# Half of the middle expert loads issued by ScalarE in a queue of its own, in a one-core mixture-of-experts kernel

## The chip, the cores and the metric

The kernel runs on one core of a Trainium2 chip. The metric is the device time of one execution in microseconds (us); lower is better. TensorE is called PE below, VectorE DVE, ScalarE ACT, GpSimd POOL and SyncE SP. "SPq" and "ACTq" are the queues in which SP and ACT issue DMA transfers.

## The reference

The program is a two-part network over a sequence of 256 rows of width 1024, all in float32. The first part is a layer with three attention-like branches, followed by a mixture of experts; the second part is four feed-forward blocks with two mixing blocks between them. The change is in the mixture of experts, which is this:

```python
N_EXPERTS = N_GROUPS * EXPERTS_PER_GROUP        # 4 * 8 = 32
D_EXPERT = 512
...
for gi in range(N_GROUPS):
    hg = jax.nn.silu(jnp.einsum('nd,edf->nef', x, wg[gi])) * jnp.einsum('nd,edf->nef', x, wu[gi])
    y = y + jnp.einsum('nef,efd->nd', hg * gates[:, gi, :, None], wd[gi])
```

Each expert has three matrices of 2 MB (gate and up 1024x512, down 512x1024), so the 32 experts are 192 MB of weights, and every one of them is read.

## The kernel before

Five programs, one for each engine, are written out by hand and are synchronised by semaphores. The experts are done in eight rounds `q` (0 to 7) of four experts each. A round has six **sets** `s`: 0 and 1 are the two halves of the gate matrices, 2 and 3 those of the up matrices, 4 and 5 those of the down matrices. A set is four loads `j` (0 to 3), one for each expert, of 128 x 2048 float32, 1 MB. This text numbers the sets through: set n is `6 * q + s`, so sets 8 and 9 are the up halves of round 1, sets 10 and 11 its down halves, and there are 48 sets, 192 loads.

What PE does in a round: `up` for sets 6q to 6q+3 (L1058), with `scatter` of the round before (L1140 and L1141) after the first of them; four transposes (L1117); `down` for sets 6q+4 and 6q+5 (L1069). In rounds 0 and 1 a `gather(q + 1)` (L939) and some transposes (L1043) follow, which build the inputs of later rounds; they need no weights. At the end of a set PE signals `("exu", q, s)`: the set is used, and its buffers are free.

What ACT does in a round, in this order: the SiLU of the gate product (L1795), which waits for PE's set 6q+1; the copy of the transposed hidden values `eT` (L1799), which waits for the transposes; in rounds 0 and 1 its half of the gather's evictions (L1774) and four copies of transposed slots (L1804); `hidden_high` (L1786), two instructions, which wait for PE's set 6q+5 and then for DVE.

Loads have fixed buffers. From set 8 to set 40 every load of set n goes into a buffer whose former content belonged to set n-4 (16 buffers in turn), so it can be issued once PE has used set n-4. SP issues all of them in the order of the sets (L3327, in `fetch`), each after its wait:

```python
if ld.prev:
    w.wait_ge(*(ld.prev.release or skey(ld.prev.final, "L")))
```

At the end the buffers are dealt out otherwise: the last load of set 41 and the first of set 42 wait for set 39, and the other three of set 42 for set 40. After set 47 come the first loads of the feed-forward block (`m<-in_ffn_w_in`).

Of the kernel before, what the change touches and what calls it, by code (L numbers as in the profile page):

```python
# [132 lines left out]
def build(nc, a, out, scr):  # L133
    with ExitStack() as ctx:
# [12 lines left out]
        signals, at, prefix = {}, {}, [""]  # L147

        def then_inc(ins, name, *keys, by=1):

            name = prefix[0] + name
            if name not in signals:
                signals[name] = Signal(ctx.enter_context(nc.semaphore(name)))
            s = signals[name]
            s.n += by
            for k in keys:
                at[k] = (s, s.n)
            ins.then_inc(s.sem, by)
# [46 lines left out]
        loads, XL, OL = [], {}, {}  # L205

        def load(dst, src, slot=None, release=None):
            if slot is None:
                kind, n = "raw", NR
                c = counts.get(kind, 0)  # L210
                counts[kind] = c + 1
                slot = (kind, c % n)
            ld = Load(len(loads), slot, tails.get(slot), dst, src, release)
            ld.raw = slots[slot]
            tails[slot] = ld
            loads.append(ld)
            return ld
# [39 lines left out]
        def expert_src(e, s):  # L257

            W = a[("expert_w_gate", "expert_w_up", "expert_w_down")[s // 2]][0, e]
            return W.rearrange("(p h k) n -> p h (k n)", p=128, h=2)[:, s % 2, :]  # L260

        def plan_experts():
            pre = [("pre", i) for i in range(7)]
            order = ex_first[:6] + pre[5:7] + ex_first[6:] + [pre[4], pre[1], pre[0], pre[2]] + ex_raw[:2] + pre[3:4]
            order += ex_raw[2:] + ex_split + (ex_first + ex_raw + ex_split) * 9
            order += ex_raw + ex_first + ex_split[:1] + ex_raw + ex_first
            for q in range(NQ):
                for s in range(6):
                    XL["set", q, s] = [load(lambda r: r, expert_src(4 * q + j, s), order.pop(0), ("exu", q, s))
                                       for j in range(4)]  # L270
            assert not order

        def plan_overflow():
            for e in range(32):
                for s in range(6):
                    OL[e, s] = load(lambda r: r, expert_src(e, s), ("over", s % 2), ("ovu", e, s))
# [16 lines left out]
        def plan_first():  # L293
# [21 lines left out]
            for c4 in range(4):  # L315
                for s in range(2):
# [14 lines left out]
        ld = load(lambda r: r[:, 0:576].rearrange("p (k n) -> p k n", n=72),  # L331
                  win[:, IK:IK + 72].rearrange("(k p) n -> p k n", p=128))
# [43 lines left out]
        s, had = 0, [None] * NH  # L376
# [11 lines left out]
        def skey(p, what):  # L388

            return (what, p.j)  # L390
# [67 lines left out]
        def ST(q):  # L458
            return rv(Sx(q, q + 1)[:, 0])
# [40 lines left out]
        for n in range(4):  # L500
            o = 24864 if n else 39456
# [62 lines left out]
            w.past = had  # L564

        where_is = {}

# [936 lines left out]
        def scalar(e, w):  # L1506
# [3 lines left out]
            def inc(ins, what, *keys):  # L1510
                then_inc(ins, "act_" + what, *keys)

            def taken(ins, *key, also=()):
                then_inc(ins, f"bank{where_is[key]}_act", ("taken", key), *also)

            def got(*key):
                w.wait_ge("full", key)
                return bank[where_is[key]]
# [261 lines left out]
            def hidden_high(q):  # L1780
                for n in range(2):
                    w.wait_ge("full", ("ed", q))
                    w.wait_ge("finf", q, n)
                    if q:
                        w.wait_ge("full", ("ey", q - 1, 1, 1))
                    inc(e.activation(fin[2 * n], sg if n else hgx, ACT.Copy), "moe", ("finH", q, n))  # L1786

            def experts():
                for q in range(NQ):
                    if q == NQ - 1:  # L1790
                        when(e, w, overflow)
                    b = got("eu", q, 0)
                    if q:
                        w.wait_ge("finL", q - 1, 1)
                    taken(e.activation(sg, b[:, :], ACT.Silu), "eu", q, 0, also=[("sg", q)])  # L1795
                    b = got("et", q)
                    if q > 1:
                        w.wait_ge("exu", q - 2, 5)
                    taken(e.activation(eT[q % 2], b[:, :], ACT.Copy), "et", q)  # L1799
                    if q < 2:  # L1800
                        gather(q + 1)
                        for s in range(4 * q, 4 * q + 4):
                            b = got("ST", s)
                            taken(e.activation(ST(s), b[:, 0:256].rearrange("p (t n) -> p t n", t=2), ACT.Copy), "ST", s)  # L1804
                    if q < NQ - 1:
                        hidden_high(q)
                e.activation(eps[:, 3:4], eps[:, 0:1], ACT.Sqrt)

            def overflow():
# [181 lines left out]
            o = 0  # L1991
# [7 lines left out]
            for ap, n in ((a["norm2_g"][0], 8), (a["ffn_norm_2"].rearrange("a b n -> (a b n)"), 32),  # L1999
# [6 lines left out]
                     by=16)  # L2006
# [1305 lines left out]
        def sync(e, w):  # L3312
            split = [0]
            fetched = set()

            def fetch(ld):

                if ld.prev:
                    w.wait_ge(*(ld.prev.release or skey(ld.prev.final, "L")))
                kind, i = ld.slot  # L3320
                if kind == "half" and i % 2 == 0:
                    kind, i = "raw", i // 2
                if ld.slot == ("pre", 6):
                    for h in range(2):
                        then_inc(e.dma_start(ld.raw[h], ld.src[:, 1024 * h:1024 * h + 1024]), "ld_pre6", ("ld", ld.n), by=16)
                else:
                    then_inc(e.dma_start(ld.dst(ld.raw), ld.src), f"ld_{kind}{i}", ("ld", ld.n), by=16)  # L3327
                fetched.add(ld.n)

            def ahead(p):  # L3330
# [95 lines left out]
            for pair in (G["wo"][-4:-2], G["wo"][-2:]):  # L3426
                i = (pair[0].slot + 1) % NH // 2
# [7 lines left out]
            for q in range(NQ):  # L3435
                for s in range(6):
                    if (q, s) == (NQ - 1, 3):
                        when(e, w, overflow)
                    if (q, s) == (NQ - 1, 5):
                        for ld in XL["set", q, s]:  # L3440
                            w.wait_ge(*ld.prev.release)
                        for i in range(2):
                            for ld in XL["set", q, s]:
                                o = slice(1024 * i, 1024 * i + 1024)
                                then_inc(e.dma_start(ld.raw[:, o], ld.src[:, o]), f"ld_{'last' if i else ''}{ld.slot[0]}{ld.slot[1]}",  # L3445
                                         ("ld", ld.n, i), by=16)
                        continue
                    for ld in XL["set", q, s]:
                        if ld.n not in fetched:
                            fetch(ld)  # L3450
            for ld in loads:
                if ld.slot[0] == "raw" and ld.prev and ld.prev.release and not ld.release:
# [103 lines left out]
```

## Time and profile before

| | before |
|---|---|
| median of 3 runs | 2061.39 us (2061.29 to 2061.7) |
| the profiled execution | 2061.97 us |
| its span in the profile | 2060.1 us |
| PE busy | 1919.6 us, 93% |
| DVE busy | 1131.3 us, 55% |
| ACT busy | 903.9 us, 44% |
| bytes read from HBM | 500.07 MB |

The span is the time between the first and the last record of the profile; the execution's own time is 1.9 us more. The experts take roughly the stretch from 617 to 1050 us of the span. There the share of PE's busy time says little, since a matmul that waits in its pipeline counts as busy; what the DMA engines moved in each stretch says more. The time of a load "to landing" runs from the start of its issue to the last of its semaphore increments, so it holds both its place behind other loads and its own transfer.

### The profile page before, as it was taken

The page shows a single profiled execution, that of the slowest core. Times are in us where ns is not written, and L with a number is a line of the kernel's source. Part 1 is how long each engine was busy: PE and PEld are TensorE (multiplying, and loading weights), DVE is VectorE, ACT ScalarE, POOL GpSimd, SP SyncE. Part 2 cuts the span into 40 slices and gives each one's busy share as a digit, 9 for nine tenths or more (in the row PEclk, how much of TensorE's full clock was granted, in tenths as well). Part 3 has the DMA queues.
Part 4 walks back from the last instruction along what each step waited for, and adds up shares of the span by engine and source line. Part 5 has one row for each costly group of instructions (what it writes and reads, how often), then busy time and mean ns, then how long its engine had stood idle before and what let it go on. Part 6 is the DMA issues. An engine that isn't in the chain of part 4 may idle for free.

```text
span 2060.1 us, 30842 instructions
## 1 busy us (share of the span) xinstructions
PE 1919.6 (93%) x12904; PEld 1492.4 (72%) x12904; DVE 1131.3 (55%) x1527; ACT 903.9 (44%) x1288; POOL 124.6 (6%) x101
## 2 busy tenths in 40 slices
PE   9999999999999876666699999999999999999998
PEld 7899988889983311111178888888888888988887
DVE  3778874578662110001156666656666766756666
ACT  4655555544342100000045546545555545675554
POOL 0243331001100000000000000000000000000000
PEclk9999999999999989889999999999999999999999
DMA  9654545678999999999985755544555555525552
GB/s 349 208 166 145 164 149 169 199 250 282 326 390 417 421 421 421 422 421 421 420 310 191 235 185 184 183 164 164 185 192 175 184 185 188 174 92 169 190 184 82
DMA packets 247506, 503.52 MB, mean 244 GB/s; under 512 B 12097, under 2 KB 166338, under 8 KB 223042
## 3 DMA queue, kind: packets, MB, share of 16 engines
q1 hardware_dynamic: 246464, 500.70, 67.7%
q8 instruction: 104, 1.70, 0.4%
q10 hardware_dynamic: 898, 0.80, 0.1%
q14 instruction: 40, 0.33, 0.0%
HBM read 500.07 MB, written 1.06 MB: 243 GB/s over the span
## 4 chain that ended last, share of the span: by engine, by line
PE 72%; DMA 10%; SPq 7%; DVE 6%; ACT 3%; issue 2%; POOL 0%; ACTq 0%; DVEq 0%
PE bank L601 14%; PE bank L662 13%; PE bank L603 13%; PE bank L602 13%; PE bank L664 7%; SPq L3327 7%; DMA m<-in_expert_w_down 4%; DMA m<-in_expert_w_up 4%; PE bank L1058 2%; DVE m L2233 1%; PE bank L1069 1%; DMA m<-in_ffn_w_in 1%; PE bank L939 1%; ACT m L1534 1%; SPq L3445 0%
## 5 line engine op out<-in xcount | busy, mean ns | idle before, releaser
L2233 DVE TENSOR_TENSOR m<-m,m 128x1024 fp32r<-128x1024 f32 x505 | 624.0, 1250 | 281.9 <-ACT m L1534 279.8
L601 PE MATMUL bank<-m,m 128*128 128x256 f32 (+1 forms) x1960 | 660.8, 337 | 6.8 <-DVE m L2233 3.4
L603 PE MATMUL bank<-m,m 128*128 128x256 f32 (+1 forms) x1960 | 646.3, 330 | 0.0
L602 PE MATMUL bank<-m,m 128*128 128x256 f32 (+1 forms) x1960 | 646.0, 330 | 0.0
L1534 ACT ACTIVATE m<-m 128x1024 fp32r<-128x1024 f32 x505 | 524.3, 1054 | 226.3 <-PE bank L603 208.7
L662 PE MATMUL bank<-m,m 128*128 128x512 f32 x1248 | 439.8, 394 | 0.0
L601 PEld LDWEIGHTS bank<-m,m 128*128 128x128 f32 x1960 | 369.3, 188 | 56.4 <-issue 10.1
L603 PEld LDWEIGHTS bank<-m,m 128*128 128x128 f32 x1960 | 369.2, 188 | 36.8
L602 PEld LDWEIGHTS bank<-m,m 128*128 128x128 f32 x1960 | 369.5, 189 | 35.4 <-issue 2.4
L664 PE MATMUL bank<-m,m 128*128 128x256 f32 x1248 | 352.7, 283 | 0.0
L662 PEld LDWEIGHTS bank<-m,m 128*128 128x128 f32 x1248 | 234.4, 188 | 54.0
L664 PEld LDWEIGHTS bank<-m,m 128*128 128x128 f32 x1248 | 234.6, 188 | 1.6
L1058 PE MATMUL bank<-m,m 128*32 128x512 f32 x1024 | 172.8, 663 | 57.0 <-DMA m<-in_expert_w_up 37.3
L1058 PEld LDWEIGHTS bank<-m,m 128*32 128x32 f32 x1024 | 40.0, 119 | 178.7 <-issue 75.6
L1884 ACT ACTIVATE m<-bank 128x256 f32<-128x256 f32 x156 | 59.0, 378 | 162.0 <-PE bank L664 162.0
L1069 PE MATMUL bank<-m,m 128*32 128x512 f32 x512 | 91.2, 671 | 35.1 <-DMA m<-in_expert_w_down 29.2
L2781 DVE TENSOR_TENSOR m<-bank,m 128x256 f32<-128x256 f32 x156 | 65.5, 422 | 59.6 <-ACT m L1884 54.8
L1069 PEld LDWEIGHTS bank<-m,m 128*32 128x32 f32 x512 | 21.7, 120 | 96.9 <-DMA m<-in_expert_w_down 57.0
L2650 DVE SCALAR_TENSOR_TENSOR m<-bank,m,m 128x512 f32<-128x512 f32 x8 | 6.0, 750 | 154.5 <-PE bank L1058 154.5
L2656 DVE TENSOR_TENSOR m<-bank,m 128x512 f32<-128x512 f32 x16 | 10.3, 685 | 140.5 <-PE bank L1069 140.5
L1799 ACT ACTIVATE m<-bank 128x512 f32<-128x512 f32 x8 | 4.8, 597 | 139.8 <-PE bank L1117 139.8
L1871 ACT ACTIVATE m<-m 128x512 fp32r<-128x512 f32 x44 | 27.8, 632 | 58.7 <-DVE m L2803 53.7
(352 smaller groups left out, 1390.7 us busy)
## 6 DMA issues: line engine op xcount, KB each, us to landing
m<-in_ffn_w_in SPq DMA_DIRECT2D x88, 1024.0 KB, 5.2
m<-in_expert_w_up SPq DMA_DIRECT2D x64, 1024.0 KB, 26.5
m<-in_expert_w_gate SPq DMA_DIRECT2D x63, 1024.0 KB, 26.3
m<-in_w_in SPq DMA_DIRECT2D x60, 1024.0 KB, 5.2
m<-in_expert_w_down SPq DMA_DIRECT2D x60, 1024.0 KB, 26.1
m<-in_ffn_w_out SPq DMA_DIRECT2D x44, 1024.0 KB, 4.9
m<-in_ada_w SPq DMA_DIRECT2D x24, 1024.0 KB, 6.5
m<-in_a_w_in SPq DMA_DIRECT2D x16, 1024.0 KB, 5.2
```

What stands on the lines that cost most here:

```text
L601: e.matmul(o, s[0], m[0], start=first, stop=False, skip_group_check=skip)
L602: e.matmul(o, s[0], m[1], start=False, stop=False, skip_group_check=skip)
L603: return e.matmul(o, s[1], m[0], start=False, stop=last, skip_group_check=skip)
L662: e.matmul(b[:, :].rearrange("p (h n) -> p h n", h=2), H, N.both[:, k], start=k == 0, stop=False, skip_group_check=True)
L664: ins = e.matmul(b[:, 0:256], L, N.T[0][:, k, :], start=False, stop=k == 7, skip_group_check=True)
L1058: ins = e.matmul(b[32 * j:32 * j + 32, :], XG(q, q + 1)[:, 0, k, 32 * j:32 * j + 32], block(ld, i), start=k == 0, stop=k == 7, skip_group_ ...
L1069: ins = e.matmul(b[n][32 * j:32 * j + 32, :], eT[q % 2][:, 128 * c + 32 * j:128 * c + 32 * j + 32], ld.raw[:, 1024 * i + 512 * n:1024 * i ...
L1534: inc(e.activation(rv(fit(q.H, q.view.shape)), q.view, ACT.Copy), "h", skey(q, "H"))
L1884: inc(e.activation(fb[6][:, 256 * b:256 * b + 256], k[:, 256:512], ACT.Copy), "ffn", (f"f{z}c", n, c, b))
L2233: inc(e.tensor_tensor(rv(fit(q.L, q.view.shape)), q.view, fit(q.H, q.view.shape), ALU.subtract), "l", skey(q, "L"))
L2781: taken(e.tensor_tensor(o, k[:, 0:256], fb[6][:, 256 * b:256 * b + 256], ALU.add), f"f{n}{z}{c}", b, also=[(f"f{z}a", n, c, b)])
L3327: then_inc(e.dma_start(ld.dst(ld.raw), ld.src), f"ld_{kind}{i}", ("ld", ld.n), by=16)
```

## The change

For sets 8 to 39, loads j = 1 and j = 3 are issued by ACT, in ACT's own DMA queue; SP keeps j = 0 and j = 2 there, and all four of the sets before 8 and from 40 on. ACT issues them at three places in each round, four loads at each: sets 6q+4 and 6q+5 after the SiLU, 6q+6 and 6q+7 after the copy `eT`, and 6q+8 and 6q+9 after `hidden_high`. Each waits for the release of the buffer's former set, as before. Buffers, bytes, sizes and PE's order are as they were. The naming of the landing semaphores is moved into functions that both engines share.

```diff
+        def of_scalar(n, j):
+
+            return 8 <= n < 40 and j % 2 == 1
...
+            def fetch_sets(n0):
+
+                for n in (n0, n0 + 1):
+                    for j in range(4):
+                        if of_scalar(n, j):
+                            ld = XL["set", n // 6, n % 6][j]
+                            done = ld.prev.release
+                            assert 6 * done[1] + done[2] <= n - 4
+                            w.wait_ge(*done)
+                            lands(e.dma_start(ld.raw, ld.src), ld)
+
             def experts():
                 for q in range(NQ):
...
                     taken(e.activation(sg, b[:, :], ACT.Silu), "eu", q, 0, also=[("sg", q)])
+                    fetch_sets(6 * q + 4)
                     b = got("et", q)
                     if q > 1:
                         w.wait_ge("exu", q - 2, 5)
                     taken(e.activation(eT[q % 2], b[:, :], ACT.Copy), "et", q)
+                    fetch_sets(6 * q + 6)
                     if q < 2:
                         gather(q + 1)
...
                     if q < NQ - 1:
                         hidden_high(q)
+                    fetch_sets(6 * q + 8)
...
-                    for ld in XL["set", q, s]:
-                        if ld.n not in fetched:
+                    for j, ld in enumerate(XL["set", q, s]):
+                        if ld.n not in fetched and not of_scalar(6 * q + s, j):
                             fetch(ld)
```

On SP, the eight loads of sets 8 and 9 stood in a row before (`L3327` is `fetch`; the names are the buffers):

```order
L3327 DMA m3_51<-in_expert_w_up 128x2048
L3327 DMA m4_52<-in_expert_w_up 128x2048
L3327 DMA m5_53<-in_expert_w_up 128x2048
L3327 DMA m29_77<-in_expert_w_up 128x2048
L3327 DMA m31_79<-in_expert_w_up 128x2048
L3327 DMA m30_78<-in_expert_w_up 128x2048
L3327 DMA m32_80<-in_expert_w_up 128x2048
L3327 DMA m24_72<-in_expert_w_up 128x2048
```

With the change, SP's eight rows at this place are sets 8 to 11, two loads of each:

```order
L3358 DMA m3_51<-in_expert_w_up 128x2048
L3358 DMA m5_53<-in_expert_w_up 128x2048
L3358 DMA m31_79<-in_expert_w_up 128x2048
L3358 DMA m32_80<-in_expert_w_up 128x2048
L3358 DMA m25_73<-in_expert_w_down 128x2048
L3358 DMA m21_69<-in_expert_w_down 128x2048
L3358 DMA m23_71<-in_expert_w_down 128x2048
L3358 DMA m1_49<-in_expert_w_down 128x2048
```

The other four loads of sets 8 and 9 have moved from SP to ACT. There, the end of round 0 and the start of round 1 stood like this before (the last of `hidden_high`, the SiLU, the copy `eT`, the gather):

```order
L1786 ACTIVATE m159_207<-m151_199 128x512
L1795 ACTIVATE m151_199<-bank1 128x512
L1799 ACTIVATE m154_202<-bank5 128x512
L1774 ACTIVATE m150_198<-bank5,m18_66 128x4x128
L1774 ACTIVATE m150_198<-bank7,m18_66 128x4x128
```

With the change it is this (L1806 is the last of `hidden_high`, L1826 the SiLU, L1831 the copy `eT`):

```order
L1806 ACTIVATE m159_207<-m151_199 128x512
L1817 DMA m4_52<-in_expert_w_up 128x2048
L1817 DMA m29_77<-in_expert_w_up 128x2048
L1817 DMA m30_78<-in_expert_w_up 128x2048
L1817 DMA m24_72<-in_expert_w_up 128x2048
L1826 ACTIVATE m151_199<-bank1 128x512
L1817 DMA m20_68<-in_expert_w_down 128x2048
L1817 DMA m22_70<-in_expert_w_down 128x2048
L1817 DMA m28_76<-in_expert_w_down 128x2048
L1817 DMA m2_50<-in_expert_w_down 128x2048
L1831 ACTIVATE m154_202<-bank5 128x512
L1817 DMA m4_52<-in_expert_w_gate 128x2048
```

So loads j = 1 and 3 of sets 8 and 9 stand behind `hidden_high` of round 0, those of sets 10 and 11 behind the SiLU of round 1, and those of sets 12 and 13 behind its copy. At the end of round 1, on ACT, loads j = 1 and 3 of sets 14 and 15 stand behind the gather (its last eviction is L1794), the slot copies (L1837) and `hidden_high`:

```order
L1794 ACTIVATE m150_198<-bank7,m18_66 128x4x128
L1837 ACTIVATE m148_196<-bank4 128x256
L1837 ACTIVATE m148_196<-bank5 128x256
L1837 ACTIVATE m148_196<-bank4 128x256
L1837 ACTIVATE m148_196<-bank5 128x256
L1806 ACTIVATE m157_205<-m152_200 128x512
L1806 ACTIVATE m159_207<-m151_199 128x512
L1817 DMA m20_68<-in_expert_w_up 128x2048
L1817 DMA m22_70<-in_expert_w_up 128x2048
L1817 DMA m28_76<-in_expert_w_up 128x2048
L1817 DMA m2_50<-in_expert_w_up 128x2048
L1826 ACTIVATE m151_199<-bank0 128x512
```

Before, they stood on SP right after set 13, with no other work ahead of them.

## Rows read from the trace of the kernel before

**Rows 1.** The page: DMA share and GB/s in 40 slices, and queue q1 (SP's).

```profile
DMA  9654545678999999999985755544555555525552
GB/s 349 208 166 145 164 149 169 199 250 282 326 390 417 421 421 421 422 421 421 420 310 191 235 185 184 183 164 164 185 192 175 184 185 188 174 92 169 190 184 82
...
q1 hardware_dynamic: 246464, 500.70, 67.7%
```

**Rows 2.** Stages: from:to, length, busy times, clock, DMA share, GB/s.

```profile
600.00:658.00 58.00, 54.82 (x657) 31.27 (x659) 18.26 (x60) 18.80 (x32) 0.00 (x0) 1.00 1.01 416
658.00:720.00 62.00, 52.31 (x323) 19.00 (x319) 12.62 (x19) 7.14 (x13) 0.00 (x0) 1.00 1.01 421
720.00:980.00 260.00, 178.41 (x902) 44.48 (x896) 24.70 (x37) 10.05 (x17) 0.00 (x0) 0.89 1.01 421
980.00:1033.00 53.00, 35.19 (x174) 8.01 (x169) 5.24 (x8) 1.77 (x3) 0.00 (x0) 0.90 1.01 419
```

**Rows 3.** Timeline of SP's DMA issues (start, length, count), 640 to 843 us.

```profile
640.77 5.19 SPq L3327 DMA_DIRECT2D m<-in_expert_w_up  x8
660.04 9.61 SPq L3327 DMA_DIRECT2D m<-in_expert_w_down  x8
...
801.91 19.84 SPq L3327 DMA_DIRECT2D m<-in_expert_w_up  x8
```

**Rows 4.** Single DMA issues and their time to landing: at 560.6, 645.5, 802.1 us.

```profile
m<-in_w_out SPq DMA_DIRECT2D x1, 1024.0 KB, 5.1
...
m<-in_expert_w_up SPq DMA_DIRECT2D x1, 1024.0 KB, 22.2
...
m<-in_expert_w_up SPq DMA_DIRECT2D x1, 1024.0 KB, 28.0
```

**Rows 5.** Timeline of PE, 656 to 710 us, and the end of set 39.

```profile
656.34 3.64 PE L1058 MATMUL bank<-m,m 128*32 128x512 f32 x32
...
664.19 10.51 PE L1058 MATMUL bank<-m,m 128*32 128x512 f32 x96
...
687.61 3.62 PE L1069 MATMUL bank<-m,m 128*32 128x512 f32 x26 [1.44 <-DMA m<-in_expert_w_down]
691.16 14.00 PE L939 MATMUL bank<-m,m 128*128 128x512 f32 x32
...
706.95 3.64 PE L1058 MATMUL bank<-m,m 128*32 128x512 f32 x32
...
967.53 3.62 PE L1058 MATMUL bank<-m,m 128*32 128x512 f32 x26 [1.43 <-DMA m<-in_expert_w_up]
```

**Rows 6.** Timeline of ACT, rounds 0 to 3, at the places of the new issues.

```profile
656.72 1.14 ACT L1786 ACTIVATE m<-m 128x512 fp32r<-128x512 f32 x2
667.90 0.60 ACT L1795 ACTIVATE m<-bank 128x512 f32<-128x512 f32 x1 [10.04 <-PE bank L1058]
676.36 0.60 ACT L1799 ACTIVATE m<-bank 128x512 f32<-128x512 f32 x1 [7.87 <-PE bank L1117]
...
707.34 1.14 ACT L1786 ACTIVATE m<-m 128x512 fp32r<-128x512 f32 x2
718.51 0.60 ACT L1795 ACTIVATE m<-bank 128x512 f32<-128x512 f32 x1 [10.04 <-PE bank L1058]
736.30 0.60 ACT L1799 ACTIVATE m<-bank 128x512 f32<-128x512 f32 x1 [17.19 <-PE bank L1117]
```

**Rows 7.** DMA issues begun between 981.4 and 981.6 us, time to landing.

```profile
m<-in_expert_w_gate SPq DMA_DIRECT2D x2, 1024.0 KB, 12.6
```

**Rows 8.** DMA traffic in the stretch 588 to 593 us.

```profile
DMA packets 293, 2.14 MB, mean 428 GB/s; under 512 B 32, under 2 KB 32, under 8 KB 32
```

**Rows 9.** DMA traffic in the stretch 671 to 683 us.

```profile
DMA packets 688, 5.01 MB, mean 417 GB/s; under 512 B 78, under 2 KB 78, under 8 KB 78
```

More of the change, by code:

```diff
@@ L564, in when, with load_signal, lands @@
             w.past = had
+        def load_signal(ld):
+            kind, i = ld.slot
+            return f"raw{i // 2}" if kind == "half" and i % 2 == 0 else f"{kind}{i}"
+        landings = {}
+        for ld in loads:
+            name = load_signal(ld)
+            landings[name] = landings.get(name, 0) + (32 if ld.slot == ("pre", 6) else 16)
+            ld.landed = landings[name]
+        def lands(ins, ld, *key):
+            name = "ld_" + load_signal(ld)
+            then_inc(ins, name, by=16)
+            at[("ld", ld.n) + key] = (signals[prefix[0] + name], ld.landed)
         where_is = {}
@@ L3319, in fetch @@
                     w.wait_ge(*(ld.prev.release or skey(ld.prev.final, "L")))
-                kind, i = ld.slot
-                if kind == "half" and i % 2 == 0:
-                    kind, i = "raw", i // 2
                 if ld.slot == ("pre", 6):
                     for h in range(2):
-                        then_inc(e.dma_start(ld.raw[h], ld.src[:, 1024 * h:1024 * h + 1024]), "ld_pre6", ("ld", ld.n), by=16)
+                        lands(e.dma_start(ld.raw[h], ld.src[:, 1024 * h:1024 * h + 1024]), ld)
                 else:
-                    then_inc(e.dma_start(ld.dst(ld.raw), ld.src), f"ld_{kind}{i}", ("ld", ld.n), by=16)
+                    lands(e.dma_start(ld.dst(ld.raw), ld.src), ld)
                 fetched.add(ld.n)
@@ L3444, in sync @@
                                 o = slice(1024 * i, 1024 * i + 1024)
-                                then_inc(e.dma_start(ld.raw[:, o], ld.src[:, o]), f"ld_{'last' if i else ''}{ld.slot[0]}{ld.slot[1]}",
-                                         ("ld", ld.n, i), by=16)
+                                half = e.dma_start(ld.raw[:, o], ld.src[:, o])
+                                if i:
+                                    then_inc(half, f"ld_last{ld.slot[0]}{ld.slot[1]}", ("ld", ld.n, 1), by=16)
+                                else:
+                                    lands(half, ld, 0)
                         continue
-                    for ld in XL["set", q, s]:
-                        if ld.n not in fetched:
+                    for j, ld in enumerate(XL["set", q, s]):
+                        if ld.n not in fetched and not of_scalar(6 * q + s, j):
                             fetch(ld)
```

## The prediction

> **What bounds the kernel now.** I read the page's slices first. From the twelfth slice to the twentieth the DMA engines are busy 9 tenths or more and move 417 to 422 GB/s; nowhere else is the figure so flat [rows 1]. Then the stages: from 658 to 980 us the DMA share is 1.01 and the rate 421 GB/s, while PE's weight loads are busy 19.0 of 62 us and 44.5 of 260 us [rows 2]. So the experts are bound by moving their bytes. A load of 1 MB (1.049 million bytes) takes 2.49 us at 421 GB/s, a set of four 10.0 us, and PE needs 3.6 us for a set whose weights are there [rows 5].
>
> Next, how SP stands to this. In the middle of the stage SP issues 8 loads in 19.84 us, 2.48 each, the pace of the engines themselves; at 640.77 it issued 8 in 5.19 us, 0.65 each [rows 3]. SP's long issues are thus back-pressure: a load issued at 802 lands 28.0 us later, and one issued at 560.6 to a queue with little in it lands 5.1 us later [rows 4]. Of the 5.1 us some 2.6 are neither waiting nor 2.49 us of transfer, and that is what a restart costs when the engines have run dry.
>
> As the stage is bound by bytes, the sum of its time is bytes by pace plus the time in which the engines have nothing to do. Before, they never run dry. The question is whether they do now.
>
> **What the change removes.** SP loses 64 of its issues. It issues at the pace of the engines because they are full, so this alone gives nothing: worth 0. The cover is the DMA share of 1.01.
>
> **What it adds on ACT.** 64 issues, four at a place, 0.4 to 0.65 us each when the queue has room: 2 to 3 us at a place. Behind them stand the SiLU, the copy `eT` or the gather's evictions. ACT had idled 10.04, 7.87 and 17.19 us ahead of such instructions [rows 6], and at most 8 loads of ACT are outstanding, fewer than the ten or so (28.0 less 2.6, by 2.49) at which SP is held back. Worth 0; if ACT were held back for 10 us at a place, PE would be late by a few us and still not the bound, as it has 6 us to spare in every set.
>
> **What it moves, first place: sets 8 and 9.** SP issued all eight at 640.77 to 646, when sets 4 and 5 were used. ACT's four now stand behind `hidden_high` of round 0, which ends at 656.72 + 1.14 = 657.9 [rows 6]. The last load of set 9, issued at 645.5, landed 22.2 us later, at 667.7 [rows 4]. With four loads fewer ahead, SP's last of set 9 lands at 667.7 - 4 x 2.49 = 657.7, and SP's next issue is at 660.04, when PE has used set 6 [rows 3, 5]. So nothing is in any queue as ACT starts. Its first load lands at 657.9 + 5.1 = 663.0 in place of 657.7 + 2.49 = 660.2: **2.8 us** lost. Bounds: 1.5 (ACT's issue meets the tail of SP's last load and part of the restart is hidden) to 3.5 (its first transfer shares the engines with SP's at once). I take 2.8.
>
> **Second place: sets 14 and 15.** Count from 663.0 - 2.49 = 660.5. Loads known to the queues by then or soon after: ACT's 8 and 9 (4), all of 10 to 13 (16), SP's 14 and 15 (4), 24 in all; the last lands at 660.5 + 24 x 2.49 = 720.3. ACT's part of 14 and 15 waits for `hidden_high` of round 1. In the trace PE ends set 11 at 687.61 + 3.62 = 691.2 and `hidden_high` ends at 708.5 [rows 5, 6], 17.3 us later, because the gather is between. When is set 11 used now? If both queues are served alike, ACT's 8 to 11 (8 loads) run beside SP's 10 to 13 (8 loads); as ACT begins 2 us sooner, its eighth is the fifteenth, landing at 660.5 + 37.3 = 697.8, up to 1.5 later with the latecomers. Set 11 is used at about 698.5 + 3.6 = 702.1, 11 us later than before, and ACT issues at 719.4; landing at 724.5, where the twenty-fifth was due at 720.3 + 2.5 = 722.8. **1.7 us** lost (bounds 0 and 2.5). SP can't help: its set 16 waits for set 12, used at 702.1 + 15.8 + 3.6 = 721.5 (the 15.8 and 3.6 are the gather and set 12 at 691.2 to 710.6 [rows 5]).
>
> The Trainium skill bears on this (DMA: Bandwidth & Descriptors, section "Queues, rings and completion order"): each DMA engine takes turns between the queues that have work, a packet at a time, which is "served alike". No row of the profile has two long queues side by side. By that rule the sum is the one above; without it, first issued first served, the second place costs nothing (below).
>
> **After that.** PE runs a set and more behind its old times, since SP's halves come four loads early and ACT's halves last. No further gap: ACT's next places follow PE's sets by 1 to 3 us, and the four loads outstanding of each queue at such times are 10 us or more.
>
> **The end of the stage.** From set 40 SP alone issues. Set 39's last load was there at 967.5 [rows 5]; now, as ACT's last, it comes some 12 us later, about 979.5 (the 11 of set 11 and the gap behind it). By then three of SP's set 40 are there too, so the lag is made up by set 41. But the fourth load of 41 and the first of 42 wait for set 39 (used at 979.5 + 3.6 = 983.1), the rest of 42 for set 40 (983.1 + 2.3 for the transposes + 3.6 = 989.0). Bytes are done about 1 us ahead of a landing, and of the 2.6 us of a restart 1.6 lie before the first byte (my split). Outstanding after 978.5 are four loads (one of 40, three of 41), which last to 988.5, against 983.1 + 1.6: a margin of 3.8 us; with two more they last to 993.4, against 989.3 + 1.6: a margin of 2.5 us. Before, a load issued at 981.5 had 12.6 us to landing [rows 7]. Worth 0, but thin. Everything behind (the halves of set 47, the feed-forward loads) keeps its order and shifts as a whole.
>
> **Sum.** 2.8 + 1.7 = +4.5 us. Against the profiled execution's 2061.97 that is 2066.5; its run was 0.6 above the median of 2061.39, so against the median: **2065.9 us**, +0.22%. A measurement of this kernel can tell about 0.2% (4.1 us) from no change, and the forecast sits on that edge, just on the slower side.
>
> **Rivals.**
> *First issued, first served* (not slower). ACT's 11 goes ahead of SP's 12 and 13: set 11 lands after twelve loads, at 660.5 + 29.9 = 690.4, is used at 694.0, and ACT issues at 711.3, with 9 us in the queues. Only the first place is left: 2061.4 + 2.8 = 2064.2. It decides when ACT's last load of set 11 lands before 696.
> *The pace rises with two queues.* For it: 588 to 593 us shows 428 GB/s [rows 8]. That is 1.7% over 325 us, -5.4 us, net 2060.5. Against: a DMA share of 1.01 leaves no gap to fill. The skill's Perfetto Trace Analysis (section "DMA Optimizations") has balancing over issuing engines help where descriptor generation is the bottleneck. By that rule SP's solid issues would speak for a gain. The 0.65 us issues [rows 3] say that generation is not the bottleneck.
> *The pace falls.* 417 GB/s is the lowest of such stretches [rows 9], 1% over 325 us, +3.1: 2069.0. The thin margins of the end, if missed by a few us, give the same.
> *Uneven service.* If SP's queue goes first, ACT's last of set 11 comes after SP's 12 to 15 too, at worst the twentieth load, 710.3, 11.8 us later than above, and the second gap grows by that: 2077.7.
> *It does nothing*: the engines don't run dry at all, as sets 6 to 9 take longer than I count: 2061.4.
>
> **How the numbers follow.** The forecast's case 0.50 (7 in 10 of it above +4.1), first served 0.17, pace up 0.12 (half of it with a gain that can be told), pace down or margins missed 0.12, uneven 0.04, nothing 0.05. Slower by over 0.2%: 0.35 + 0.12 + 0.04 = 0.51. Faster: 0.06. Same: 0.43. The range leaves out the uneven case and the better half of "pace up": 2061.0 to 2070.0; the likeliest case alone is 2064.5 to 2067.5.
>
> **What the profile would show.** The GB/s near 658 to 661 and again near 719 to 723 falls below 421; the issue on ACT behind `hidden_high` of round 0 lands about 5 us later; SP's long issues of 2.1 us vanish between sets 8 and 39; PE's waits fall on j = 1 and 3, some 10 us later than before until set 39, and it catches up by set 41; the stage ends 4 to 5 us late. The prediction is wrong if the rate stays flat at both places, if ACT's issues are held back by SP's, or if a third gap opens near 983 to 990.

## The result, and the profile after

| | before | after |
|---|---|---|
| time, median (us) | 2061.88 | 2065.23 |
| runs, from-to (us) | 20, 2060.49 to 2063.43 | 20, 2063.36 to 2068.87 and one of 2399.49 |
| profiled execution (us) | 2061.97 | 2065.36 |
| its span (us) | 2060.1 | 2063.5 |
| granted clock over the span | 0.983 | 0.970 |

The ratio is 1.0016 with an interval of [1.001, 1.0023]: the change costs 3.35 us, between 2 and 5. Single runs in a slow state (2399.49 us here, one of 2174.61 in e2, one of 3094.74 of the kernel before beside e1 to e4) are left out of the comparisons.

The page of the changed kernel, its GB/s in 40 slices and its two queues, q1 of SP and q10 of ACT:

```profile
GB/s 351 206 165 145 164 147 169 199 251 280 326 385 398 413 422 421 422 421 420 420 322 204 234 184 184 184 160 167 184 188 180 184 184 186 173 92 170 192 184 82
...
q1 hardware_dynamic: 237248, 433.58, 59.4%
q10 hardware_dynamic: 10114, 67.91, 8.0%
```

SP's queue carries 67.1 MB less than before (500.70 MB) [rows 1], and ACT's queue as much more: 67.91 MB, where it had 0.80. Two slices are low that were not: the thirteenth (398, was 417) and the fourteenth (413, was 421), of 51.6 us each. The others of the stage read 420 to 422, as before.

The stages of the changed kernel (from:to, length, busy times, clock, DMA share, GB/s):

```profile
600.00:658.00 58.00, 54.82 (x652) 32.13 (x654) 19.25 (x61) 18.18 (x33) 0.00 (x0) 1.00 1.00 411
658.00:720.00 62.00, 48.38 (x260) 16.15 (x261) 9.55 (x14) 7.86 (x16) 0.00 (x0) 0.89 1.00 408
720.00:980.00 260.00, 169.57 (x934) 46.35 (x928) 27.59 (x42) 10.14 (x18) 0.00 (x0) 0.82 1.01 420
980.00:1033.00 53.00, 36.44 (x200) 9.14 (x196) 5.99 (x9) 2.36 (x4) 0.00 (x0) 0.89 1.01 420
```

Against [rows 2] the long stretch from 720 to 980 us has the same pace. Stretches of 5 us find the places:

```profile
655.00:660.00 5.00, 4.40 (x32) 1.96 (x34) 1.64 (x3) 2.91 (x7) 0.00 (x0) 1.00 0.69 244
660.00:665.00 5.00, 3.37 (x22) 1.23 (x14) 2.24 (x4) 0.00 (x0) 0.00 (x0) 1.00 0.98 408
...
715.00:720.00 5.00, 4.29 (x29) 1.91 (x31) 1.13 (x2) 2.93 (x7) 0.00 (x0) 1.00 1.04 390
720.00:725.00 5.00, 4.07 (x30) 1.37 (x20) 2.23 (x4) 0.09 (x1) 0.00 (x0) 1.00 0.91 369
```

What counts is the last number, the GB/s, and the one ahead of it, the DMA share, which falls to 0.69 near 658 us and to 0.91 near 722. A stretch of 5 us at a rate r has lost 5 x (421 - r) / 421 us. That gives 2.10 + 0.15 = 2.25 us at the first place and 0.37 + 0.62 = 0.99 at the second, 3.24 us together, beside 3.35 measured. That the two agree so well is partly luck: 2065.23 is a median of many runs, and the 3.24 us are of one execution. That execution had moved 0.66 MB less than the one of before by 600 us, ahead of every issue that was moved, which is 1.6 us at 421 GB/s. The stage added 3.3 us, and some 1.5 us were gone again by the end (the table of the experiments has the same for each). From 975 to 1000 us all stretches are at 418 to 426: there is no third gap.

The first gap in stretches of 1 us:

```profile
657.00:658.00 1.00, 0.76 (x8) 0.52 (x12) 0.00 (x0) 0.75 (x4) 0.00 (x0) 1.00 0.50 205
658.00:659.00 1.00, 1.00 (x12) 0.30 (x13) 0.01 (x1) 1.00 (x4) 0.00 (x0) 1.00 0.14 41
659.00:660.00 1.00, 1.00 (x12) 0.26 (x8) 1.00 (x2) 0.41 (x1) 0.00 (x0) 1.00 0.85 156
```

It is a dip with slopes and not a pause: 393 GB/s before it, 336 and 418 in the two stretches behind it.

The arithmetic with stretches of 5 us serves for every experiment below, with the low stretches of its own trace.

ACT's timeline in the changed kernel at the three kinds of place (start, length, then what it waited for; ACTq is ACT issuing DMAs):

```profile
658.11 0.36 ACTq L1817 DMA_DIRECT2D m<-in_expert_w_up  x1
658.27 0.62 ACT L1806 ACTIVATE m<-m 128x512 fp32r<-128x512 f32 x1
658.50 0.51 ACTq L1817 DMA_DIRECT2D m<-in_expert_w_up  x1
658.79 0.62 ACT L1806 ACTIVATE m<-m 128x512 fp32r<-128x512 f32 x1
659.04 1.91 ACTq L1817 DMA_DIRECT2D m<-in_expert_w_up  x2
...
669.44 0.60 ACT L1826 ACTIVATE m<-bank 128x512 f32<-128x512 f32 x1 [10.03 <-PE bank L1078]
669.45 1.81 ACTq L1817 DMA_DIRECT2D m<-in_expert_w_down  x4
...
681.86 0.60 ACT L1831 ACTIVATE m<-bank 128x512 f32<-128x512 f32 x1 [11.82 <-PE bank L1137]
681.87 1.78 ACTq L1817 DMA_DIRECT2D m<-in_expert_w_gate  x4
...
718.79 0.34 ACTq L1817 DMA_DIRECT2D m<-in_expert_w_up  x1
```

L1806 is `hidden_high`, L1826 the SiLU, L1831 the copy `eT`, L1817 the new issue. The first issue, at 658.11, starts ahead of the `hidden_high` that stands before it in the program. Those at 669.45 and 681.87 begin together with the activation in front of them, not after it. The landing of the issue at 658.11 and of that at 718.79, from the DMA issues of the changed kernel (the last number is us from issue to landing):

```profile
m<-in_expert_w_up ACTq DMA_DIRECT2D x1, 1024.0 KB, 5.4
...
m<-in_expert_w_up ACTq DMA_DIRECT2D x1, 1024.0 KB, 5.1
```

Both are the time of a load in an idle queue [rows 4]. SP's timeline in the middle of the stage, from 792.6 to 793.5 us:

```profile
792.66 0.80 SPq L3358 DMA_DIRECT2D m<-in_expert_w_gate  x2
```

SP now issues two loads in 0.80 us where it took 2.48 for one [rows 3]: the back-pressure is gone from its queue, and its share of the chain that ended last falls from 7% to 1%. The pace of the bytes did not notice. PE's timeline in the changed kernel around sets 8 to 12 and near 980 us:

```profile
676.62 3.62 PE L1078 MATMUL bank<-m,m 128*32 128x512 f32 x26 [2.96 <-DMA m<-in_expert_w_up]
...
696.51 6.34 PE L1089 MATMUL bank<-m,m 128*32 128x512 f32 x26 [3.74 <-DMA m<-in_expert_w_down]
702.78 14.00 PE L959 MATMUL bank<-m,m 128*128 128x512 f32 x32
...
976.86 6.12 PE L1078 MATMUL bank<-m,m 128*32 128x512 f32 x26 [4.20 <-DMA m<-in_expert_w_up]
985.46 4.57 PE L1089 MATMUL bank<-m,m 128*32 128x512 f32 x38 [0.89 <-ACT m L1831]
```

Set 11 is used at 702.8 (696.51 + 6.34), where it was 691.2 [rows 5]. The waits ahead of a set's last matmuls are 3 to 4 us, since ACT's j = 1 and 3 come last, and some of those 26 matmuls take 6.1 to 6.3 us in place of 3.6.

In the middle of the stage the two queues are served alike. Traffic of the changed kernel from 780 to 790 us (packets, MB, share):

```profile
q10 hardware_dynamic: 289, 2.09, 50.5%
q1 hardware_dynamic: 287, 2.08, 50.0%
```

### The profile page after: what moved, and what is told of

The parts are those of the page before. It is cut to its first block, busy times and chain, and to the rows that moved or that the text cites. A ratio compares the mean times of both kernels' runs of the same rounds, so it can differ in the third digit from the quotient of the medians.

```text
span 2063.5 us, 30842 instructions
## 1 busy us (share of the span) xinstructions
PE 1911.2 (93%) x12904; PEld 1493.2 (72%) x12904; DVE 1130.3 (55%) x1527; ACT 904.0 (44%) x1288; POOL 126.3 (6%) x101
## 3 DMA queue, kind: packets, MB, share of 16 engines
q10 hardware_dynamic: 10114, 67.91, 8.0%
## 4 chain that ended last, share of the span: by engine, by line
PE 72%; DMA 14%; DVE 7%; ACT 4%; issue 2%; SPq 1%; ACTq 0%; POOL 0%; DVEq 0%
PE bank L682 13%; PE bank L621 13%; PE bank L623 13%; PE bank L622 13%; PE bank L684 7%; DMA m<-in_expert_w_up 5%; DMA m<-in_expert_w_down 5%; PE bank L1078 3%; DMA m<-in_expert_w_gate 2%; DVE m L2267 2%; PE bank L959 1%; PE bank L1089 1%; DMA m<-in_ffn_w_in 1%; ACT m L1554 1%; DVE m L2389 0%
## 5 line engine op out<-in xcount | busy, mean ns | idle before, releaser
L621 PEld LDWEIGHTS bank<-m,m 128*128 128x128 f32 x1960 | 368.8, 188 | 56.8 <-DVE m L2267 10.3
L1078 PE MATMUL bank<-m,m 128*32 128x512 f32 x1024 | 166.8, 712 | 66.7 <-DMA m<-in_expert_w_up 46.5
L1089 PE MATMUL bank<-m,m 128*32 128x512 f32 x512 | 89.1, 759 | 37.2 <-DMA m<-in_expert_w_down 31.3
L2690 DVE TENSOR_TENSOR m<-bank,m 128x512 f32<-128x512 f32 x16 | 10.3, 686 | 140.4 <-PE bank L1089 140.4
L1831 ACT ACTIVATE m<-bank 128x512 f32<-128x512 f32 x8 | 4.8, 597 | 144.6 <-PE bank L1137 144.6
```

The costliest lines, as they stand in the source:

```text
L621: e.matmul(o, s[0], m[0], start=first, stop=False, skip_group_check=skip)
L1078: ins = e.matmul(b[32 * j:32 * j + 32, :], XG(q, q + 1)[:, 0, k, 32 * j:32 * j + 32], block(ld, i), start=k == 0, stop=k == 7, skip_group_ ...
L1089: ins = e.matmul(b[n][32 * j:32 * j + 32, :], eT[q % 2][:, 128 * c + 32 * j:128 * c + 32 * j + 32], ld.raw[:, 1024 * i + 512 * n:1024 * i ...
```

## The experiments

Each edits the changed kernel and ran beside the kernel before, whose median was 2061.73 us beside e1 to e4, 2061.29 beside e5 and e6, and 2061.87 beside e7 to e9. "Measured" is the difference of the medians. The other columns are of the one profiled execution of each kernel, against that of before. "Lost" is worked out from the 5 us stretches. "Start" and "stage" go by bytes: what the execution had moved less than that of before (136.54 MB) by 600 us, and from 600 to 1023 us (before: 177.78 MB), at 421 GB/s. "Whole" is the difference of the two executions' times.

| kernel | measured (us) | ratio, interval | lost (us) | start (us) | stage (us) | whole (us) |
|---|---|---|---|---|---|---|
| the change | +3.35 | 1.0016 [1.001, 1.0023] | 3.2 | +1.6 | +3.3 | +3.4 |
| e1_sp_keeps_8_9 | +1.05 | 1.0005 [0.9996, 1.0014] | 3.2 | -0.5 | +3.1 | +1.0 |
| e2_sp_keeps_14_15 | +2.55 | 1.0013 [1.0004, 1.0022] | 2.9 | 0.0 | +2.9 | +1.4 |
| e3_ahead_of_gather | +0.76 | 1.0002 [0.9994, 1.0011] | 2.3 | +0.5 | +2.2 | +0.6 |
| e4_one_queue_late | +3.93 | 1.0019 [1.001, 1.0028] | 4.0 | +1.0 | +3.8 | +3.2 |
| e5_acts_8_9_later | +10.82 | 1.0049 [1.0035, 1.0063] | 10.0 | +2.1 | +9.7 | +10.3 |
| e6_ahead_of_gather_to_36 | +1.32 | 1.0005 [0.9996, 1.0014] | 0 | +1.7 | 0.0 | +0.6 |
| e7_sp_issues_all | +0.19 | 1.0001 [0.9992, 1.001] | 0 | +0.6 | +0.1 | +0.7 |
| e8_to_36_again | +0.63 | 1.0003 [0.9994, 1.0012] | 0 | +0.3 | +0.1 | +1.2 |
| e9_sets_12_to_35 | +0.53 | 1.0002 [0.9993, 1.0011] | 1.0 | +1.6 | +0.9 | +1.0 |

In every trace the stage grew by what its low stretches had lost, within 0.2 us, except e5 with 0.3.

My theory: time is lost where both queues run empty, and that is a matter of when the moved loads are issued. The first rival: a second queue costs something in itself.

### e1_sp_keeps_8_9: SP keeps sets 8 and 9

```diff
         def of_scalar(n, j):
-            return 8 <= n < 40 and j % 2 == 1
+            return 10 <= n < 40 and j % 2 == 1
```

> SP issues all loads of sets 8 and 9 again; ACT has j = 1 and 3 of sets 10 to 39. My theory (the change costs the time in which both queues are empty, near 658 and near 720 us): no gap near 658, and since ACT's halves then lag by about 2 loads in place of 4, set 11 is used at about 695 in place of 702, so ACT's issue at the end of round 1 comes at about 712 with some 5 us still in the queues: no gap there either. Time as before, +0.0 (within 0.7 us), with 60 issues still in ACT's queue. Rival A (a second queue costs pace, or ACT's issues cost its other work, in proportion to their number): 60 of 64 stay, so +3.1 of the +3.3 us. Rival B (each late place costs by itself): the second place still costs, +1.0.

Measured +1.05 us, where +0.0 within 0.7 was expected. Its 5 us stretches:

```profile
655.00:660.00 5.00, 4.40 (x32) 1.96 (x34) 1.63 (x3) 2.92 (x7) 0.00 (x0) 1.00 1.01 423
...
665.00:670.00 5.00, 4.95 (x30) 1.56 (x34) 0.69 (x1) 0.00 (x0) 0.00 (x0) 0.66 0.96 401
670.00:675.00 5.00, 5.00 (x52) 1.34 (x48) 0.00 (x0) 0.60 (x1) 0.00 (x0) 1.00 0.69 241
...
715.00:720.00 5.00, 4.69 (x38) 1.63 (x38) 1.30 (x2) 2.22 (x6) 0.00 (x0) 1.00 0.98 356
```

The gap near 658 is gone, as the theory has it, but another has opened near 671 that I had missed. In this trace ACT issues its part of sets 10 and 11 here:

```profile
671.01 1.92 ACTq L1817 DMA_DIRECT2D m<-in_expert_w_down  x4
```

They stand behind the SiLU of round 1, which waits for set 7, whereas SP issued all of set 10 as soon as set 6 was used (660.04 [rows 3]). Until then the queues hold set 9 and SP's half of set 10. In the changed kernel the first gap has already put the landings later against PE, and this place holds. The gap near 716 is left too. The expectation had it gone, as set 11 would be used sooner; it fits a gap that only sets 14 and 15 make.

The size of the gap near 671 is that of this execution. PE's matmuls of sets 4 and 5 took 8.77 us where they took 7.07 before (from 637.07):

```profile
636.89 8.77 PE L1089 MATMUL bank<-m,m 128*32 128x512 f32 x64 [0.69 <-ACT m L1831]
```

The granted clock was 0.77 from 635 to 640 us and 0.66 from 665 to 670 (the line above), against 1.00 before in both. So the gather of round 0 began at 645.59, 1.5 us later than before, though the bytes were 0.5 us early, and set 7 was used 9.45 us after set 6 and not 7.86 as before. In all PE stood some 3.6 us worse against the bytes than before. ACT asked at 671.0, 0.8 us ahead of the last landing (671.8). At full clock it would by these dates have asked 4.4 us ahead of it, and the change lost nothing near 989 us, where an ask came 4.8 us ahead: an estimate, by which most of this gap would not be there. How large the gap is in the other executions of e1, whose median is +1.05 us, no trace shows.

### e2_sp_keeps_14_15: SP keeps sets 14 and 15

```diff
-            return 8 <= n < 40 and j % 2 == 1
+            return 8 <= n < 40 and n not in (14, 15) and j % 2 == 1
```

> SP issues all loads of sets 14 and 15; ACT has j = 1 and 3 of sets 8 to 13 and 16 to 39. My theory: the gap near 658 stays as it is (about 2.2 us of moved bytes lost between 655 and 665), the one near 720 goes, since SP issues four loads more by about 703. Time +2.2 us against before (1.6 to 2.8). Rival A (in proportion to the issues): +3.1. Rival B (what counts is the lag of ACT's halves, not the empty queues; it is still 4 loads): +3.3.

Measured +2.55 us, inside the expected 1.6 to 2.8. Its 5 us stretches:

```profile
655.00:660.00 5.00, 4.40 (x41) 1.60 (x39) 1.29 (x2) 2.91 (x7) 0.00 (x0) 1.00 0.57 177
...
715.00:720.00 5.00, 4.29 (x38) 1.72 (x40) 1.29 (x2) 3.02 (x7) 0.00 (x0) 1.00 1.01 419
720.00:725.00 5.00, 3.31 (x20) 1.27 (x8) 1.97 (x3) 0.00 (x0) 0.00 (x0) 1.00 1.02 418
```

The second gap closes and the first stays (2.9 us here). So the second gap comes from sets 14 and 15 behind the gather, and their return to SP, with 30 sets still shared, leaves the first gap alone. The difference to the change, 0.8 us, is smaller than the intervals; the closed gap is the evidence, not the time.

### e3_ahead_of_gather: ACT issues these sets ahead of the gather

```diff
                     if q < 2:
+                        fetch_sets(6 * q + 8)
                         gather(q + 1)
...
-                    fetch_sets(6 * q + 8)
+                    if q >= 2:
+                        fetch_sets(6 * q + 8)
```

> All 64 loads stay with ACT, but in rounds 0 and 1 its third place (sets 8 and 9, 14 and 15) stands ahead of its gather evictions in place of behind hidden_high, so that it issues as soon as sets 4, 5 (about 645) and 10, 11 are used. My theory: no stretch with both queues empty, time as before, +0.0 (within 0.7 us). Rival A (second queue or ACT's issues cost): +3.3. Rival C (two queues are faster by themselves, hidden so far by the gaps): -1 to -5 us.

Measured +0.76 us, a little above the expected 0.0 within 0.7. Its 5 us stretches read 424 and 423 at the two places of the change, but these are low:

```profile
670.00:675.00 5.00, 5.00 (x52) 1.53 (x48) 0.00 (x0) 0.60 (x1) 0.00 (x0) 1.00 0.95 352
...
985.00:990.00 5.00, 5.00 (x42) 1.80 (x38) 0.00 (x0) 0.00 (x0) 0.00 (x0) 0.85 0.86 318
990.00:995.00 5.00, 2.51 (x20) 0.63 (x10) 2.22 (x4) 1.17 (x2) 0.00 (x0) 1.00 0.97 398
```

The dip near 671 is e1's once more: here too PE's 64 matmuls of sets 4 and 5 took 8.77 us, which no other trace shows. PE's timeline in this kernel near 980 us:

```profile
974.16 6.34 PE L1078 MATMUL bank<-m,m 128*32 128x512 f32 x26 [3.87 <-DMA m<-in_expert_w_up]
...
982.98 9.53 PE L1089 MATMUL bank<-m,m 128*32 128x512 f32 x64 [0.89 <-ACT m L1831]
```

The first is the end of set 39: its last weights are there at 974.16, but the 26 matmuls take 6.34 us, not 3.62. Set 40 behind it is slow as well and is used at 988.35, 7.8 us after set 39, where the prediction has 5.9 (the change: 6.1). The loads asked for at the end of set 39 landed without a break, the last at 991.3. What came late is the next ask, of the three loads of set 42 that wait for set 40: 3.0 us before that landing, where the change asked 4.8 us before. So it is the second of the prediction's margins (2.5 us) that failed, and both sets in it were slower than the 3.6 us on which it rests.

### e4_one_queue_late: one queue, and loads 1 and 3 of sets 8 and 9 issued late

```diff
-            return 8 <= n < 40 and j % 2 == 1
+            return False
...
                     if 6 * q + s == 10:
+                        w.wait_ge("finH", 0, 1)
+                        for n in (8, 9):
+                            for j in (1, 3):
+                                fetch(XL["set", n // 6, n % 6][j])
...
-                        if ld.n not in fetched and not of_scalar(6 * q + s, j):
+                        if ld.n not in fetched and not (6 * q + s in (8, 9) and j % 2):
```

SP issues everything; the four loads of the first place only go after `hidden_high` of round 0.

> ACT issues none; SP issues all in one queue, as before, but loads j = 1 and 3 of sets 8 and 9 only after hidden_high of round 0 has ended (about 658), with everything behind them in SP's order after that. My theory (late issue is the cost, the second queue is not): the queue is empty from about 657 on, as with the change, and the first late load lands about 5 us after its issue: +2.8 us (2.2 to 3.5), a little more than the first gap of the change, as ACT's queue had issued 1 us before hidden_high ended; no gap near 720. Rival A (a second queue costs): +0.0 to +0.5.

Measured +3.93 us, with a single queue, above the expected 2.2 to 3.5. Its stretches:

```profile
655.00:660.00 5.00, 4.40 (x35) 1.89 (x37) 1.54 (x3) 2.91 (x7) 0.00 (x0) 1.00 0.36 149
660.00:665.00 5.00, 3.30 (x19) 1.40 (x12) 1.97 (x3) 0.00 (x0) 0.00 (x0) 1.00 0.99 360
...
720.00:980.00 260.00, 177.52 (x920) 43.99 (x919) 25.42 (x38) 10.64 (x18) 0.00 (x0) 0.91 1.01 421
```

3.23 + 0.72 = 3.95 us are lost at one place. The first rival falls for this term: late issue costs it, with no second queue about. It costs more than in the change (2.25), by 1.7 us, and the dates account for it. SP really waits for `hidden_high` to end and issues at 659.05, while ACT's DMA instructions start ahead of it (658.11): 0.9 us. And SP's last load of set 9 had landed at 658.4, in the change at 659.3: the queue was empty 0.9 us sooner.

### e5_acts_8_9_later: the first place made worse

```diff
+                    if q == 1:
+                        fetch_sets(8)
                     fetch_sets(6 * q + 4)
...
-                    fetch_sets(6 * q + 8)
+                    if q:
+                        fetch_sets(6 * q + 8)
```

> As the change, but ACT's loads of sets 8 and 9 stand behind the SiLU of round 1 (near 669) in place of behind hidden_high of round 0 (near 658), together with its loads of sets 10 and 11. My theory (the time follows the stretches with both queues empty): data stop at about 658, SP's first two loads of set 10 bring them back from about 663 to 668, then nothing until about 671: 7 to 8 us lost by 672 where the change loses 2.3; near 720 up to 1 us. In all +8.5 us against before (7 to 10). Rival (the cost is that ACT issues and a second queue are there at all): +3.3 as with the change. Rival (lag of ACT's halves, capped by the buffers): little more than the change, +3.5 to +4.5.

Measured +10.82 us, just above the expected range of 7 to 10. Its stretches:

```profile
655.00:660.00 5.00, 4.40 (x27) 2.25 (x29) 0.81 (x2) 2.84 (x8) 0.00 (x0) 1.00 0.58 239
660.00:665.00 5.00, 4.22 (x30) 1.49 (x22) 2.24 (x4) 0.28 (x1) 0.00 (x0) 1.00 0.29 69
665.00:670.00 5.00, 4.08 (x35) 1.34 (x35) 1.58 (x3) 0.00 (x0) 0.00 (x0) 1.00 0.84 351
670.00:675.00 5.00, 1.09 (x6) 0.11 (x1) 0.00 (x0) 0.60 (x1) 0.00 (x0) 0.96 0.73 251
...
725.00:730.00 5.00, 4.68 (x38) 1.43 (x36) 1.58 (x3) 1.69 (x4) 0.00 (x0) 1.00 0.96 356
```

Lost: 2.16 + 4.18 + 0.83 + 2.02 + 0.77 = 9.96 us. Gaps three times as large give a time three times as large; what comes later in the program takes back only some 1.4 us (start and stage against whole, in the table).

### e6_ahead_of_gather_to_36, e8_to_36_again: no gap left

```diff
-            return 8 <= n < 40 and j % 2 == 1
+            return 8 <= n < 36 and j % 2 == 1
```

on top of the edit of e3; e8 is the same kernel once more.

> As the run with the issues ahead of the gather, but ACT's share ends with set 35 (56 loads in place of 64). There the rate fell only at 985 to 990 us (318 GB/s, 1.3 us lost with 398 behind it), where SP's loads of sets 41 and 42 wait for sets 39 and 40 while PE lags. With ACT's share ended four sets sooner the lag is made up by set 37, so my theory expects 418 or more in every 5 us from 640 to 1030 and a time as before: +0.0 (within 0.7). Rival (a second queue or a lower granted clock of PE costs by itself): +0.8, as measured with the issues ahead of the gather.

> The same program as the one with the issues ahead of the gather and ACT's share ended with set 35, which measured +1.3 us with an interval of -0.8 to +2.9 though no stretch of it fell below 411 GB/s. My theory: +0.0 to +0.5, so that the two together hold 0. Rival (56 issues in ACT's queue, or the lower granted clock of PE, cost 1 us and more without a gap): +1.3 again, and above the control of this call by as much.

No 5 us stretch of e6 from 655 to 1033 us is below 410 (before: 411). Measured +1.32 and +0.63 us, where +0.0 within 0.7 and +0.0 to +0.5 were expected; each is not to be told from 0. The two medians, 2062.61 and 2062.50, differ less than those of the kernel before beside them. So 112 of the 128 loads of sets 8 to 39 are still shared by two queues, no gap is left, and of the 3.35 us there remain 0.6 to 1.3 that can't be told from 0. The long stretch of e8:

```profile
720.00:980.00 260.00, 176.40 (x943) 45.76 (x946) 25.43 (x38) 10.64 (x18) 0.00 (x0) 0.82 1.01 421
```

### e7_sp_issues_all: the control

```diff
-            return 8 <= n < 40 and j % 2 == 1
+            return False
```

> The changed program with ACT's share set to none: SP issues all loads in the order of before. A control for the way the comparison is made. My theory: no stretch below 411 GB/s from 640 to 1030 us, time as before, +0.0 (within 0.5). If it is slower or faster by 1 us, the runs so far are to be read against it and not against before.

Measured +0.19 us. The rest of the changed code costs nothing that can be told. Against this control, which ran beside them, e8 is 0.44 us slower and e9 0.34. The long stretch of e7, for the clock beside e8's:

```profile
720.00:980.00 260.00, 179.97 (x938) 43.73 (x934) 24.73 (x37) 10.64 (x18) 0.00 (x0) 0.90 1.01 421
```

### e9_sets_12_to_35: the second queue only from set 12

```diff
-            return 8 <= n < 36 and j % 2 == 1
+            return 12 <= n < 36 and j % 2 == 1
```

on top of e6.

> As the run before it in this list, with ACT's share from set 12 to set 35 (48 loads), so that SP keeps sets 8 to 11 as well: there a gap was left in the runs that kept only 8 and 9 with SP (241 GB/s at 670 to 675), as ACT's part of set 10 waits for the SiLU of round 1 and so for set 7 in place of set 6. My theory: no gap, +0.0 (within 0.7). Rival (in proportion to ACT's issues, 1.3 for 56): +1.1.

Measured +0.53 us. No gap was expected, but it has one low stretch, about 1 us worth:

```profile
730.00:735.00 5.00, 5.00 (x52) 1.38 (x48) 0.00 (x0) 0.60 (x1) 0.00 (x0) 1.00 0.91 339
```

It doesn't beat the kernel before either. No version did, and by the theory none should: before, there was no dry stretch in the expert stage to fill [rows 1, 2], and the pace with two queues is no higher.

## Why the prediction was right, point by point

**The sum** was +4.5 us, 2065.9; measured were +3.35 and 2065.23, inside the likeliest case's own range both as a time and as a difference (+3.1 to +6.1). At 0.16%, with 0.2% inside its interval, it stands on the edge that the forecast named, just on the other side of it. The mechanism held at both places, but that the difference comes so near to the forecast is partly luck: both terms were too large, 4.5 us against 3.24 lost, and some 1.5 us of what the stage lost are given back later, which the working leaves out. What made up for it in the profiled execution is its start, 1.6 us late. The likeliest case's lower end of 2064.5 isn't worked out either: the bounds of the two terms add up to 2062.9 to 2067.4.

**What it removes: 0.** Right. SP's long issues vanished between sets 8 and 39 (from 640 to 960 us one is over 1 us, where 107 were), and the pace stayed at 420 GB/s; they were a symptom of full engines.

**ACT's own issues: 0.** Right: four issues take 1.8 us (669.45, 681.87), 0.45 each, and the SiLU and `eT` start beside them.

**First place: 2.8 us, bounds 1.5 to 3.5.** Right in mechanism; it measured 2.25. The working had ACT's first ask 0.2 us behind the last landing of set 9 (657.9 and 657.7). ACT's first DMA instruction started at 658.11, 0.16 us before its first `hidden_high` activation and 1.3 us ahead of the end on which I had counted; the last landing was at 659.3, 1.2 us behind the ask. With these dates the prediction's arithmetic would have given 658.11 + 5.4 - (659.27 + 2.49) = 1.8 us, so the restart itself costs more than a count by landings says: the bytes thin out ahead of the last landing and come back slowly, as the stretches of 1 us show. e4, where the ask came 0.7 us behind the last landing, lost 3.95, above my upper bound of 3.5. e5 tripled the gaps and the time followed.

**Second place: 1.7 us, bounds 0 to 2.5.** Right in mechanism (e2 closes it), 1.0 in size. Set 11 was used at 702.8 where I had 702.1, and ACT issued at 718.8 where I had 719.4, but these dates hold by luck. The last load of set 11 landed at 696.5 where I had 698.5, although the expert stage started about 1.5 us later in this execution (PE's gather near the end of round 0 began at 645.62, before at 644.07); its last 26 matmuls took 6.34 us where I had 3.6; and ACT asked 1.3 us ahead of the end of `hidden_high`. By landings there is no gap at all here: ACT's load came at 723.9, 2.5 us behind the last one in the queues (721.4). What was lost are the slopes. The Trainium skill's turn-taking between queues (DMA: Bandwidth & Descriptors, "Queues, rings and completion order") is what the trace shows: 50.5 and 50.0% of the traffic.

**The end of the stage: 0, but thin.** Right for the change (no low stretch near 985), and thin indeed: e3, with the two gaps of the change closed, lost 1.5 us there. The date of set 39 held in the same way as that of set 11: its last load was there at 976.9 where I had 979.5, its matmuls took 6.1 us where I had 3.6, and it was used at 983.0 where I had 983.1. The step that was off is PE's 3.6 us for a set: with two queues its last 26 matmuls often take 6 us and more, at a lower granted clock. My split of the restart, 1.6 us before the first byte and 1 us behind the last, was off too: a load alone in its queue (issued at 1078.1 in the trace of before, 5.1 us to landing) has its first packet 1.0 us after the issue and its last 0.5 us before the landing, and the other 1.1 us are slopes at both ends.

**The rivals.** *First issued, first served* is dead. The test that I had set for it is too close to count, 696.5 against 696 in an execution that started 1.5 us late, but the order of landing decides: SP's first load of set 12, issued at 672.87, landed at 691.9, ahead of ACT's last of set 11, issued at 670.81 and landed at 696.5. And the second gap is there. *The pace rises*: 420 against 421 in the long stretch, dead. By the Trainium skill (Perfetto Trace Analysis, "DMA Optimizations") balancing over issuing engines helps where descriptor generation is the bottleneck; with a DMA share of 1.01 before and 0.40 us an issue after, it was not, and the trace agrees. *The pace falls*: not by rate. *Uneven service*: dead by the shares. *Nothing*: dead, by both gaps.

**What is left open.** In the traces of the change, of e1 to e5 and of e9, start and stage together are 1.4 to 2.1 us more than the whole, in e6 1.1, in e7 nothing, and in e8 0.8 less. So a part of the delay is taken back behind 1045 us, where the program is no longer bound by bytes; what does it I did not seek. Less these 1.5 us the gaps of the change would cost 1.8 us, a little below its measured interval of 2.1 to 4.7. The start may make up the rest: it is later than before in eight of the ten traces, by up to 2.1 us and 0.9 in the mean, ahead of every issue that was moved. With one trace of before it can't be said whether that is the kernel or the execution. Every one of the nine measured above what the theory expected for it, and e6, e8 and e9, with little or no gap, stand at +0.5 to +1.3. A cost of up to 1 us of the second queue, or of the changed program, is neither shown nor excluded.

## What to carry to other kernels

Where the DMA engines were busy without a break, handing half of the issues to another engine did not make the bytes faster: an issue of 2.1 us was the queue's back-pressure and not SP's work. What it changes is the date of each ask, since a DMA placed in a compute engine's program waits for whatever that program waits for. Go through every such place and compare the date of the ask with the last landing of what the queues still hold then. In these traces an ask 4.8 us ahead of that landing cost nothing (the change near 989 us), 3.0 us ahead 1.5 us (e3), 2.6 us ahead 1.0, 1.2 us ahead 2.25 (both in the change), and 0.7 us behind it 3.95 (e4). Do this again after closing one gap, because the next low point, which the first delay had covered, can open (985 us in e3; 671 us in e1 and e3, there with PE late by its clock as well). And leave room for a compute engine that runs slower than in the trace of before.

## What was unexpected of the hardware

**ACT's DMA instructions run ahead of its activations.** The issue at 658.11 began before the two activations that stand in front of it (658.27, 658.79), by 1.3 us to the end of the second.

**The granted clock of PE is lower with two queues.** From 720 to 980 us it is 0.82 in the change and in e8 and 0.82 to 0.85 in the other six kernels with two queues, against 0.89 before [rows 2], 0.90 in e7 and 0.91 in e4, at the same GB/s. The clock has two levels, 1.2 and 2.4 GHz; the means lie between them. What differs in PE's rows ahead of the slow stretches is its idle time: ACT's and SP's loads land in pairs, about 5 us apart, so a wait is 3 to 4 us where it was 1.4 [rows 5], and some of the 26 matmuls behind it take 6.1 to 6.3 us in place of 3.6. Whether the pairing causes the lower clock I have not tested. It costs the change nothing that shows, since PE has time to spare in every set, but it used up the margin near 985 us in e3. The low clock near 637 us in e1 and e3 is something else: there the loads of both kernels were still all SP's.

**A restart is a slope.** The rate in the first gap of the change goes 393, 205, 41, 156, 336, 418 GB/s in six stretches of 1 us. A gap that the landings don't show at all (the second, with landings 2.5 us apart) still cost 1.0 us of bytes.
